# Moving half output maps of the S5 branch from GpSimd to VectorE, earlier, in a fused attention + SSM + FFN layer

## The chip, the cores and the metric

The kernel runs on one core of one Trainium2 chip. The metric is the device time of one execution in microseconds (us), as the median of several runs. The core has five engines that run side by side and meet only at semaphores: TensorE (PE, matmuls; its weight loads are listed as PEld), VectorE (DVE), ScalarE (ACT), GpSimd (POOL) and SyncE (SP, which here only issues DMAs).

## The reference

One layer of a hybrid encoder, 16 meta tokens ahead of 512 tokens, model width 1024, all in float32:

```python
xn = rmsnorm(h, norm1_g)
q, k, v, u, gates = split(xn @ w_in)          # 4 heads of 64; u is 512 wide; gates 2 x 1024
q, k = rmsnorm(q, q_norm_g), rmsnorm(k, k_norm_g)     # per head
attn = stick_breaking_attention(q, k, v)
y = s5_ssm(u, ...)                            # 32 groups of 16 channels, 64 complex states each
g = gelu(y); ssm = g * sigmoid(g @ w_glu + b_glu)
h = h + (sigmoid(gate_a) * (attn @ w_attn_proj) + sigmoid(gate_s) * (ssm @ w_ssm_proj)) @ w_o
up = causal_dwconv3(rmsnorm(h, norm2_g) @ w_up)
h = h + (silu(gate_f) * val_f) @ w_down       # FFN width 2816
```

The S5 recurrence is x[t] = A x[t-1] + B u[t], y[t] = Re(C x[t]) + D u[t], with A diagonal and complex.

## The kernel before

Tokens lie on the free axis, so an activation is stored as 8 tiles of 128 channels by 528 tokens. Every product with a weight matrix is done in three float32 products (high by high, high by low part, low by high) and cut into **units**: one unit is 128 output channels, 48 matmuls of 252 or 264 columns. Units 0 to 3 give u, 4 and 5 K, 6 and 7 Q, 8 and 9 V, 10 to 24 and 27 the gates, 25 and 26 the GLU, 28 to 35 the two projections, 36 to 43 W_o; the FFN follows. The weights go through two slots, even and odd units: SP loads `raw`, ACT rounds it to `hi` (L925), VectorE makes `lo` = `raw` - `hi` (L1309), and PE waits for `lo_ready` ahead of each unit. ACT may overwrite a slot of `hi` only when the unit two before is done, so `lo` of unit n+2 can be made only while unit n+1 runs on PE.

Each engine walks the same list of units. At unit n, VectorE first makes `lo` of unit n+2 (`split`) and then does the steps that `STEPS[n]` lists, in order; ACT first evacuates unit n, then rounds `hi` of unit n+2, then does its steps; PE runs unit n and then its steps; SP loads the weights of unit n+2 and then does `MOVES[n]`. No engine looks ahead: what stands behind a wait in its list waits as well. GpSimd has one list of its own, written out at the end of its block.

The S5 branch is worked in 4 rounds of 4 pairs of groups, in chunks of 8 tokens, beside units 8 to 16:

- the **input map** of a round (`g_in`, GpSimd, `input_map`) and its **output map** (`hout`, `map_part`), each with a real and an imaginary half. One half map is 3 multiplies or adds of 128x576 (L499, L500, L501) from the powers `pw` and from `ct`. There are three buffers `hout`, so the map of round 3 waits until round 0 has been read out
- `prep` r: PE turns the input map and multiplies the output map into the taps (waits `g_ready`, `h_pool`, `h_dve`); ACT copies `win` and `kern` (L1037, `kern_raw`); VectorE adds the skip term (L1507, `kern_set`); SP spreads the taps over `toep` in 8 DMAs (L540, `kern_out`)
- `state` r: PE (L1949), then VectorE's rotation and scan (L1528 to L1542), which sets `xst` (`st_set`)
- `readout` r: PE multiplies the taps (L1961) and the states (L1970); it waits for `kern_out`, for `st_set`, and for the last users of banks 6 and 7, which are the copy of `kern` and the two copies of V (`vl_set`, L1552) of `turn_v`. `y_ps` says that it is done

Before the change GpSimd makes the imaginary halves (`parts=(1,)`) of rounds 0, 1 and 2 and both of round 3; VectorE makes the real halves of rounds 0, 1 and 2 in units 6, 7 and 8 (the step `out_map`), with `mod` as scratch, for which it waits until all of u has been written (`u_out`). The step `norms` of unit 9 is, on VectorE, the Newton step of the q and k norms (L1315 to L1317, `rows_set`); SP's `norm_write` and `norm_read` of units 11 and 12 move its result, and `scale` uses it in unit 12. After its maps GpSimd makes masks and then restores the residual, `hT` times `rb` in 8 instructions (L892), for W_o.

Of the kernel before, what the change touches and what calls it, by code (L numbers as in the profile page):

```python
# [23 lines left out]
P = 128  # L24
# [7 lines left out]
KD = D // P  # L32
# [3 lines left out]
GROUPS, GH, ST = 32, 16, 64  # L36
# [8 lines left out]
T8 = 8  # L45
NC = L // T8
RP = PAIRS // 4
ROUNDS = 4
# [50 lines left out]


STEPS = {0: [("angle", 0)], 1: [("angle", 1)], 2: [("columns", 0), ("angle", 2)],
         3: [("turns", 0)], 4: [("columns", 1), ("turns", 1)],
         5: [("square", 0)], 6: [("square", 1), ("out_map", 0)],
         7: [("square", 2), ("out_map", 1)], 8: [("square", 3), ("out_map", 2), ("prep", 0)],
         9: [("state", 0), ("norms", 0)],
         10: [("prep", 1), ("turn_v", 0)], 11: [("readout", 0), ("state", 1)],
         12: [("prep", 2), ("turn_v", 1)] + [("scale", i) for i in range(4)], 13: [("readout", 1), ("state", 2)],
         14: [("prep", 3), ("turn_v", 2)], 15: [("readout", 2), ("state", 3), ("head", 0)],
         16: [("head", 1), ("readout", 3)],
# [18 lines left out]
NORM_TILE = 32  # L128
TURN_BANK = 7
HOUTS = 3  # L130


ROW_ARE, ROW_AIM, ROW_STEP, ROW_SKIP = 0, 32, 64, 96
# [33 lines left out]
def hybrid_trunk(nc, x, meta_tokens, norm1_g, w_in, q_norm_g, k_norm_g, ssm_a_re, ssm_a_im,  # L167
# [8 lines left out]
    with ctx:  # L176
        def alloc(stack, name, shape, dt=F32):
            return stack.enter_context(nc.sbuf_tensor(name, shape, dt))
# [4 lines left out]
        def sem(name):  # L183
            return ctx.enter_context(nc.semaphore(name))
# [31 lines left out]
        HOUT = 2 * RP * (T8 + 1) * GH  # L216
        v_at = hout_end - HOUTS * HOUT - 2 * L
        vT = [gates[:, v_at + i * L:v_at + (i + 1) * L] for i in range(2)]
# [5 lines left out]
        ma = [alloc(mix, f"ma{i}", [P, LL]) for i in range(2)]  # L224
        mb = [alloc(mix, f"mb{i}", [P, LL]) for i in range(2)]
        pad = alloc(mix, "pad", [P, 4 * (L - LL)])
        v2 = alloc(mix, "v2", [P, 5, HEADS, 2 * DH], F32R)
        skips = ExitStack()
        skip_i = alloc(skips, "skip_i", [GH, GROUPS, GH])
# [16 lines left out]
        mod = alloc(early, "mod", [P, 4, RP, NC])  # L246
# [9 lines left out]

        hout = [gates[:, hout_end - (HOUTS - i) * HOUT:hout_end - (HOUTS - 1 - i) * HOUT]
                .rearrange("p (c r n h) -> p c r n h", c=2, r=RP, h=GH) for i in range(HOUTS)]
        kern = alloc(early, "kern", [GH, 2 * RP, P])
# [100 lines left out]
        pw_set = sem("pw_set")  # L360
# [4 lines left out]
        h_pool = sem("h_pool")  # L365
        h_dve = sem("h_dve")
# [6 lines left out]
        u_out = [sem(f"u_out{i}") for i in range(ROUNDS)]  # L373
# [5 lines left out]
        st_set = sem("st_set")  # L379
        y_ps = sem("y_ps")  # L380
# [108 lines left out]
        def map_part(eng, link, r, c, t, n=RP):  # L489

            shape = [P, n, T8 + 1, GH]
            t = t[:, 0:n * (T8 + 1) * GH].rearrange("p (r n h) -> p r n h", r=n, h=GH)
            for r0 in range(0, RP, n):
                pr = slice(r * RP + r0, r * RP + r0 + n)
                a = [pw[:, i, :, pr].rearrange("p n r -> p r n").unsqueeze(3).broadcast_to(shape)
                     for i in range(2)]
                b = [ct[:, i, pr, :].unsqueeze(2).broadcast_to(shape) for i in range(2)]
                o = hout[r % HOUTS][:, c, r0:r0 + n]
                link(eng.tensor_tensor(o, a[0], b[c], ALU.mult))  # L499
                link(eng.tensor_tensor(t, a[1], b[1 - c], ALU.mult))  # L500
                link(eng.tensor_tensor(o, o, t, ALU.subtract if c else ALU.add))  # L501
# [8 lines left out]
        def linker(eng, link):  # L510

            count = [0]

            def wait_for(ins):
                count[0] += 1
                ins.then_inc(link, 1)
                eng.wait_ge(link, count[0])
            return wait_for
# [28 lines left out]
        def _(sp):  # L547
# [97 lines left out]
            def y_read(_):  # L645
                for r in range(ROUNDS):
                    sp.wait_ge(y_out[r], 16)
                sp.wait_ge(st_set, ROUNDS)
                sp.wait_ge(y_ps, ROUNDS)
                for g in range(2 * RP):  # L650
                    sp.dma_start(yT[GH * g:GH * (g + 1)].rearrange("p r j c -> p (r j) c"),
                                 y_dram[:, :, :, g].rearrange("r j h c -> h (r j) c"))\
                        .then_inc(y_in, 16)
# [9 lines left out]
            def rms_read(_):  # L663

                sp.wait_ge(rms_out, 32)
                sp.dma_start(rb[:], rms_dram.partition_broadcast(P)).then_inc(rb_in, 16)
# [66 lines left out]
        def _(pool):  # L733
            link = linker(pool, pool_link)
# [87 lines left out]
            def input_map(r):  # L822

                if r >= 2:
                    pool.wait_ge(g_t, r - 1)
                n = RP if r < 2 else RP // 2
                shape = [P, n, T8, GH]
                for r0 in range(0, RP, n):
                    pr = slice(r * RP + r0, r * RP + r0 + n)
                    cmul(pool, link, both(g_in[r % 2][:, :, r0:r0 + n]),  # L830
                         [pw[:, c, 0:T8, pr].rearrange("p n r -> p r n").unsqueeze(3)
                          .broadcast_to(shape) for c in range(2)],
                         [bb[:, c, pr, :].unsqueeze(2).broadcast_to(shape) for c in range(2)],
                         tmp(n, T8, GH))
                pool.nop().then_inc(g_ready, 1)

            def output_map(r, parts=(1,)):

                if r >= HOUTS:
                    pool.wait_ge(y_ps, r - HOUTS + 1)  # L840
                for c in parts:
                    map_part(pool, link, r, c, pt, RP if r < 2 else RP // 2)
                pool.nop().then_inc(h_pool, 1)

# [15 lines left out]
                             .broadcast_to([P, PAIRS, NC - 1])).then_inc(decay_set, 1)  # L860
            output_map(1)
            input_map(1)
            output_map(2)
            input_map(2)
            input_map(3)
            output_map(3, (0, 1))

            tri = pt[:, 0:P]
            link(pool.memset(tri, -1.0))
# [19 lines left out]

            pool.wait_ge(rb_in, 16)  # L890
            for k in range(KD):
                pool.tensor_tensor(hT[:, k, :], hT[:, k, :], rb[:], ALU.mult).then_inc(h_raw, 1)  # L892
            for m in range(KD):
                pool.wait_ge(m_gated, m + 1)
# [408 lines left out]
        def _(dve):  # L1303
            link = linker(dve, dve_link)
# [8 lines left out]
            def newton(r, v, t, factor=1.0):  # L1313

                link(dve.scalar_tensor_tensor(t, v, -0.5 * factor, r, ALU.mult, ALU.mult))  # L1315
                link(dve.tensor_tensor(t, t, r, ALU.mult))
                return dve.scalar_tensor_tensor(r, t, 1.5 * factor, r, ALU.add, ALU.mult)  # L1317
# [107 lines left out]
                dve.scalar_tensor_tensor(xl[:, k], hT[:, k], g1[:, k:k + 1], xh[:, k].bitcast(F32),  # L1425
                                         ALU.mult, ALU.subtract).then_inc(x_ready, 1)

            def out_map(r):

                if r >= HOUTS:  # L1430
                    dve.wait_ge(y_ps, r - HOUTS + 1)
                if r == 0:
                    dve.wait_ge(pw_set, 1)
                    for u in u_out:
                        dve.wait_ge(u, 16)
                map_part(dve, link, r, 0, mod_flat)
                dve.nop().then_inc(h_dve, 1)

            mod_flat = mod[:].rearrange("p i r c -> p (i r c)")

            def rounded(o, n):

# [43 lines left out]
                                                None, ALU.mult)  # L1486
                ins.then_inc(ct_set, 1)

            def norms(_):

                dve.wait_ge(rs_a, 1)
                newton(row_r, row_v, row_t).then_inc(rows_set, 1)
# [175 lines left out]
            def evacuate(unit):  # L1668
# [2 lines left out]
                dve.tensor_copy(*unit_tile(unit)).then_inc(gate_late, 1)  # L1671

            steps = {"columns": columns, "out_map": out_map, "angle": angle, "turns": turns,
                     "norms": norms, "scale": scale, "prep": prep, "state": state,
                     "head": head,
                     "scores": scores, "suffix": suffix, "values": values, "gelu": gelu,
                     "turn_v": turn_v}
# [131 lines left out]
        def _(pe):  # L1809
# [109 lines left out]
            def prep(r):  # L1919

                pe.wait_ge(g_ready, r + 1)
                for c in range(2):
                    for i in range(RP):
                        ins = pe.transpose(ps[:, 4 + c, i * P:(i + 1) * P],
                                           g_in[r % 2][:, c, i].rearrange("p j h -> p (j h)"), ident[:])
                ins.then_inc(g_t, 1)
                pe.wait_ge(h_pool, r + 1)
                pe.wait_ge(h_dve, min(r + 1, HOUTS))
                for k in range(RP // 2):
                    for c in range(2):  # L1930
                        for half in range(2):
                            i = 2 * k + half
                            p0 = ST * half
                            ins = pe.matmul(ps[p0:p0 + 3 * GH, 6, k * P:(k + 1) * P],
                                            bpair[:, c, r * RP + i, :],
                                            hout[r % HOUTS][:, c, i, 0:T8, :]
                                            .rearrange("p i h -> p (i h)"),
                                            start=c == 0, stop=c == 1)
                ins.then_inc(k_ps, 1)
# [333 lines left out]
            for half in range(2):  # L2273
                pe.wait_ge(lo_ready, U_END - 1 + half)
                for c in range(2):
                    t = slice(2 * P * c, 2 * P * (c + 1))
                    for i in range(UT):
                        k = half * UT + i
# [33 lines left out]
```

## Time and profile before

| | us |
|---|---|
| median of 3 runs (706.46, 706.69, 709.88) | 706.69 |
| the profiled execution | 707.04 |
| its span, first to last instruction | 705.3 |
| PE busy | 694.5 (98%) |
| VectorE busy | 422.4 (60%) |
| ScalarE busy | 322.0 (46%) |
| GpSimd busy | 184.3 (26%) |

The span is cut into 40 equal slices on the page; each digit is the busy share of a slice in tenths, and PEclk is the granted TensorE clock. The stretch of this case is slices 3 to 8, some 50 to 155 us.

```profile
PE   9999989989999999999999999999999999999998
DVE  5775989687777756445766666666666662322221
POOL 7899999920000023231101010101101010000000
```

Most of the chain that ended last is PE's products; the same page puts 90% of it on PE and 4% on VectorE.

### The profile page before, as it was taken

How to read it: one execution, taken by the hardware profiler on the slowest of the kernel's cores; microseconds unless marked ns; L12 is line 12 of the kernel's file. 1: busy time of each engine (PE TensorE's matmuls, PEld its weight loads, DVE VectorE, ACT ScalarE, POOL GpSimd, SP SyncE). 2: the span in 40 equal slices, each digit the busy share in tenths (PEclk: the TensorE clock that was granted, in tenths of full speed). 3: DMA queues.
4: the chain of work that ended last, by engine and by line, in shares of the span. 5: the costliest groups of instructions: out<-in, count | busy, mean ns of one | idle time of the engine just before them, and what ended most of it. 6: DMA issues, size and time to landing. Idle time of an engine off the chain costs nothing.

```text
span 705.3 us, 14227 instructions
## 1 busy us (share of the span) xinstructions
PE 694.5 (98%) x5680; PEld 662.4 (94%) x5680; DVE 422.4 (60%) x559; ACT 322.0 (46%) x483; POOL 184.3 (26%) x209
## 2 busy tenths in 40 slices
PE   9999989989999999999999999999999999999998
PEld 7899979989999999999999999999999998888887
DVE  5775989687777756445766666666666662322221
ACT  4754543668889653445444444444343432111220
POOL 7899999920000023231101010101101010000000
PEclk9999999999999999999999999999999999999999
DMA  8168344249211234333333333333333342333331
GB/s 232 47 186 135 78 124 135 64 139 114 70 60 53 68 91 121 90 91 90 90 91 90 89 89 89 91 91 99 98 96 90 100 124 82 98 97 97 97 98 46
DMA packets 139930, 69.26 MB, mean 98 GB/s; under 512 B 23476, under 2 KB 137880, under 8 KB 139888
## 3 DMA queue, kind: packets, MB, share of 16 engines
q1 hardware_dynamic: 139727, 68.65, 36.7%
q8 instruction: 30, 0.49, 0.3%
q14 instruction: 13, 0.10, 0.0%
q10 hardware_dynamic: 160, 0.02, 0.0%
HBM read 63.19 MB, written 4.28 MB: 96 GB/s over the span
## 4 chain that ended last, share of the span: by engine, by line
PE 90%; DVE 4%; ACT 2%; issue 2%; SPq 1%; DMA 1%; POOL 0%; DVEq 0%; ACTq 0%; POOLq 0%
PE ps L1814 80%; PE ps L1841 1%; PE ps L2017 1%; PE ps L2067 1%; PE ps L1865 1%; DVE lo L1309 1%; PE ps L1970 1%; PE ps L2034 1%; ACT xh L994 1%; PE ps L1961 1%; DVE mod L500 1%; SPq L540 1%; DVE gates L499 1%; DVE gates L501 1%; PE ps L1874 1%
## 5 line engine op out<-in xcount | busy, mean ns | idle before, releaser
L925 ACT ACTIVATE hi<-raw 128x1024 fp32r<-128x1024 f32 (+2 forms) x102 | 111.5, 1094 | 244.2 <-PE ps L1814 226.6
L1814 PE MATMUL ps<-xh,hi 128*128 128x264 f32 (+1 forms) x1088 | 219.5, 283 | 0.1
L1814 PE MATMUL ps<-xl,hi 128*128 128x264 f32 (+1 forms) x1088 | 218.7, 282 | 0.0
L1309 DVE TENSOR_TENSOR lo<-raw,hi 128x1024 fp32r<-128x1024 f32 (+2 forms) x102 | 135.5, 1328 | 138.9 <-ACT hi L925 138.3
L1814 PE MATMUL ps<-xh,lo 128*128 128x264 f32 (+1 forms) x1088 | 218.0, 282 | 0.0
L1814 PEld LDWEIGHTS ps<-xh,hi 128*128 128x128 f32 x1088 | 167.3, 189 | 1.5 <-issue 0.6
L1814 PEld LDWEIGHTS ps<-xl,hi 128*128 128x128 f32 x1088 | 166.8, 188 | 0.0
L1814 PEld LDWEIGHTS ps<-xh,lo 128*128 128x128 f32 x1088 | 166.6, 188 | 0.0
L908 POOL TENSOR_TENSOR cv<-cv 128x512 f32<-128x512 f32 x22 | 28.3, 1289 | 226.7 <-DVE cv L1766 226.7
L1814 PE MATMUL ps<-ah,hi 128*128 128x512 f32 (+1 forms) x198 | 74.3, 375 | 0.0
L1814 PE MATMUL ps<-al,hi 128*128 128x512 f32 (+1 forms) x198 | 73.1, 369 | 0.0
L1814 PE MATMUL ps<-ah,lo 128*128 128x512 f32 (+1 forms) x198 | 72.9, 368 | 0.0
L1766 DVE SCALAR_TENSOR_TENSOR cv<-ut,cols,cv 128x512 f32<-128x512 f32 x88 | 65.9, 749 | 7.6 <-DVE cv L1766 2.7
L1755 DVE TENSOR_TENSOR ut<-ps,rb 128x516 f32<-128x516 f32 x44 | 30.6, 695 | 61.4 <-PE ps L1814 61.3
L1814 PEld LDWEIGHTS ps<-ah,lo 128*128 128x128 f32 x198 | 37.2, 188 | 7.3
L895 POOL TENSOR_TENSOR ma<-ma,mb 128x516 f32<-128x516 f32 x8 | 10.9, 1359 | 125.2 <-DVE mb L1711 125.2
L1814 PEld LDWEIGHTS ps<-ah,hi 128*128 128x128 f32 x198 | 37.2, 188 | 6.6
L1814 PEld LDWEIGHTS ps<-al,hi 128*128 128x128 f32 x198 | 37.3, 188 | 6.5
L1254 ACT ACTIVATE cv<-ut,cols 128x512 f32<-128x512 f32 x44 | 35.6, 808 | 1.8 <-DVE ut L1755 1.6
L1261 ACT ACTIVATE cv<-cv 128x512 f32<-128x512 f32 x22 | 13.9, 633 | 34.5 <-DVE cv L1766 34.5
L1814 PE MATMUL ps<-mh,hi 128*128 128x264 f32 (+1 forms) x128 | 25.7, 282 | 0.5 <-DVE ml L1695 0.3
L1814 PE MATMUL ps<-ml,hi 128*128 128x264 f32 (+1 forms) x128 | 25.8, 283 | 0.0
(298 smaller groups left out, 956.0 us busy)
## 6 DMA issues: line engine op xcount, KB each, us to landing
raw<-in_w_up_dram SPq DMA_DIRECT2D x88, 256.0 KB, 3.1
raw<-in_w_in_dram SPq DMA_DIRECT2D x52, 256.0 KB, 3.4
raw<-in_w_down_dram SPq DMA_DIRECT2D x16, 384.0 KB, 3.5
raw<-in_w_down_dram SPq DMA_DIRECT2D x16, 320.0 KB, 4.0
raw<-in_w_o_dram SPq DMA_DIRECT2D x16, 256.0 KB, 3.0
xtok<-in_x_dram SPq DMA_DIRECT2D x4, 512.0 KB, 5.5
raw<-in_w_ssm_proj_dram SPq DMA_DIRECT2D x8, 256.0 KB, 2.8
out_dram<-yt SPq DMA_DIRECT2D x7, 256.0 KB, 2.4
```

Source lines behind the costliest of these rows:

```text
L499: link(eng.tensor_tensor(o, a[0], b[c], ALU.mult))
L500: link(eng.tensor_tensor(t, a[1], b[1 - c], ALU.mult))
L501: link(eng.tensor_tensor(o, o, t, ALU.subtract if c else ALU.add))
L895: pool.tensor_tensor(ma[m % 2][:], ma[m % 2][:], mb[m % 2][:], ALU.add)\
L908: pool.tensor_tensor(cv[s][:, 1], cv[s][:, 0], cv[s][:, 1], ALU.mult)\
L925: act.activation(hi[slot][:, 0:n * P], raw[slot][:, 0:n * P], ACT.Copy)\
L1254: act.activation(cv[s][:, part], ut[s][:, part, 2:2 + SEQ], ACT.Identity, bias=cols[:, bass.ds(m + COL_CB, 1)], scale=cols[:, bass.ds(m + ...
L1261: act.activation(cv[s][:, 0], cv[s][:, 0], ACT.Silu).then_inc(silu_a, 1)
L1309: dve.tensor_tensor(lo[slot][:, 0:n * P], raw[slot][:, 0:n * P], hi[slot][:, 0:n * P].bitcast(F32), ALU.subtract)\
L1755: dve.tensor_tensor(ut[s_][:, part], joined(4 * s_ + 2 * part, CUT_LATE), rb[:, 0:LL], ALU.mult).then_inc(up_v, 1)
L1766: dve.scalar_tensor_tensor(cv[s_][:, part], ut[s_][:, part, 2 + tap:2 + tap + SEQ], w, cv[s_][:, part], ALU.mult, ALU.add)\
L1814: ins = pe.matmul(o, weights[w], acts(a, c), start=start and i == 0, stop=stop and i == 2)
```

## The change

It moves work between engines and within VectorE's list; what is computed stays the same.

- VectorE makes four half maps instead of three: the real halves of rounds 0, 1 and 2 and the imaginary half of round 2. They stand in units 4, 5, 6 and 7 instead of 6, 7 and 8. The scratch is a new tile `map_tmp` in the place where `v2` (the turned V) lies later, so the wait for `u_out` is gone.
- GpSimd makes the imaginary halves of rounds 0 and 1 and both of round 3. `output_map(2)` is gone from its list.
- PE's waits in `prep` follow that split (`POOL_MAPS`, `DVE_MAPS`).
- VectorE's Newton step of the norms, now called `rates`, moves from unit 9 (behind `state` 0) to unit 10, behind `prep` 1 (the taps' skip term) and `turn_v` 0.
- GpSimd's residual restore waits for `st_set` of all four rounds ahead of its fifth instruction.

```diff
-         3: [("turns", 0)], 4: [("columns", 1), ("turns", 1)],
-         5: [("square", 0)], 6: [("square", 1), ("out_map", 0)],
-         7: [("square", 2), ("out_map", 1)], 8: [("square", 3), ("out_map", 2), ("prep", 0)],
+         3: [("turns", 0)], 4: [("columns", 1), ("turns", 1), ("out_map", 0)],
+         5: [("square", 0), ("out_map", 1)], 6: [("square", 1), ("out_map", 2)],
+         7: [("square", 2), ("out_map", 3)], 8: [("square", 3), ("prep", 0)],
          9: [("state", 0), ("norms", 0)],
-         10: [("prep", 1), ("turn_v", 0)], 11: [("readout", 0), ("state", 1)],
+         10: [("prep", 1), ("turn_v", 0), ("rates", 0)], 11: [("readout", 0), ("state", 1)],
+MAPS_HERE = ((0, 0), (1, 0), (2, 0), (2, 1))
+MAPS_THERE = {0: (1,), 1: (1,), 3: (0, 1)}
+DVE_MAPS, POOL_MAPS = (1, 2, 4, 4), (1, 2, 2, 3)
+        maps = ExitStack()
+        map_tmp = alloc(maps, "map_tmp", [P, RP * (T8 + 1) * GH])
+        maps.close()
         v2 = alloc(mix, "v2", [P, 5, HEADS, 2 * DH], F32R)
...
-            def output_map(r, parts=(1,)):
+            def output_map(r):
...
-                for c in parts:
+                for c in MAPS_THERE[r]:
                     map_part(pool, link, r, c, pt, RP if r < 2 else RP // 2)
...
             output_map(1)
             input_map(1)
-            output_map(2)
             input_map(2)
             input_map(3)
-            output_map(3, (0, 1))
+            output_map(3)
...
             for k in range(KD):
+                if k == KD // 2:
+                    pool.wait_ge(st_set, ROUNDS)
                 pool.tensor_tensor(hT[:, k, :], hT[:, k, :], rb[:], ALU.mult).then_inc(h_raw, 1)
...
-            def out_map(r):
-                if r >= HOUTS:
-                    dve.wait_ge(y_ps, r - HOUTS + 1)
-                if r == 0:
-                    dve.wait_ge(pw_set, 1)
-                    for u in u_out:
-                        dve.wait_ge(u, 16)
-                map_part(dve, link, r, 0, mod_flat)
+            def out_map(i):
+                r, c = MAPS_HERE[i]
+                dve.wait_ge(pw_set, 1)
+                map_part(dve, link, r, c, map_tmp)
                 dve.nop().then_inc(h_dve, 1)
...
-            def norms(_):
+            def rates(_):
                 dve.wait_ge(rs_a, 1)
                 newton(row_r, row_v, row_t).then_inc(rows_set, 1)
...
-                pe.wait_ge(h_pool, r + 1)
-                pe.wait_ge(h_dve, min(r + 1, HOUTS))
+                pe.wait_ge(h_pool, POOL_MAPS[r])
+                pe.wait_ge(h_dve, DVE_MAPS[r])
```

## Rows read from the trace of the kernel before

**Rows 1.** Waits of PE, whole span: us in total, times, longest.

```profile
PE ps L1961 <- issue: 2.9, 1, 2.9
```

**Rows 2.** Windows: start:end, length, busy us of each engine, PEclk, DMA.

```profile
102.40:107.30 4.90, 4.90 (x129) 4.58 (x129) 1.01 (x1) 1.88 (x3) 4.41 (x6) 0.65 0.81 241
121.30:124.70 3.40, 3.40 (x130) 3.16 (x129) 2.68 (x3) 0.63 (x2) 3.16 (x4) 1.00 0.02 5
```

**Rows 3.** Timeline, end of unit 11: start, duration, instruction, [idle before <- releaser].

```profile
98.40 1.52 ACT L1037 ACTIVATE kern<-ps 16x256 f32<-16x256 f32 x4
99.56 1.74 DVE L1309 TENSOR_TENSOR lo<-raw,hi 128x1024 fp32r<-128x1024 f32 x1
101.22 0.72 DVE L1507 TENSOR_TENSOR kern<-kern,skip_i 16x128 f32<-16x128 f32 x1
101.87 0.41 DVE L1552 TENSOR_TENSOR v<-ps,v 128x256 fp32r<-128x256 f32 x1
102.38 1.66 PE L1961 MATMUL ps<-uc,toep 128*64 128x66 f32 x32 [2.90 <-issue]
```

**Rows 4.** Timeline, SP's queue, ACT and VectorE ahead of that.

```profile
86.60 5.61 SPq L540 DMA_DIRECT2D toep<-kern  x8
92.25 2.24 SPq L556 DMA_DIRECT2D raw<-in_w_in_dram  x4
96.25 1.25 DVE L1315 SCALAR_TENSOR_TENSOR gates<-gates 128x528 f32<-128x528 f32 x1
96.48 1.06 ACT L925 ACTIVATE hi<-raw 128x1024 fp32r<-128x1024 f32 x1 [4.35 <-DMA raw<-in_w_in_dram]
```

**Rows 5.** Timeline, VectorE, units 4 to 7.

```profile
57.49 1.12 DVE L1471 TENSOR_SCALAR rot<-rot 128x1056 f32<-128x1056 f32 x1
59.85 2.19 DVE L1309 TENSOR_TENSOR lo<-raw,hi 128x1024 fp32r<-128x1024 f32 x1 [1.25 <-ACT hi L925]
65.50 1.53 DVE L1309 TENSOR_TENSOR lo<-raw,hi 128x1024 fp32r<-128x1024 f32 x1 [3.46 <-ACT hi L925]
72.13 2.21 DVE L1309 TENSOR_TENSOR lo<-raw,hi 128x1024 fp32r<-128x1024 f32 x1 [0.15 <-DVE gates L501]
```

**Rows 6.** Windows from first to last instruction of two of VectorE's half maps.

```profile
66.95:71.98 5.03, 5.03 (x44) 5.03 (x43) 4.96 (x4) 2.17 (x4) 4.87 (x4) 1.00 0.20 23
81.26:85.90 4.64, 4.64 (x69) 3.81 (x68) 4.54 (x4) 1.87 (x4) 4.30 (x4) 1.00 0.01 4
```

**Rows 7.** Timeline, PE: first matmul of units 7, 8 and 9.

```profile
63.71 0.28 PE L1814 MATMUL ps<-xh,hi 128*128 128x252 f32 x1
69.42 0.29 PE L1814 MATMUL ps<-xh,hi 128*128 128x264 f32 x1
77.25 0.39 PE L1814 MATMUL ps<-xh,hi 128*128 128x264 f32 x1
```

**Rows 8.** Timeline: `state` 2 and 3 on VectorE, GpSimd's restore, `readout` 3.

```profile
127.22 0.70 DVE L1528 TENSOR_TENSOR mod<-ps,rot 128x528 f32<-128x528 f32 x1
132.29 0.77 DVE L1542 TENSOR_TENSOR xst<-mod 128x260 f32<-128x260 f32 x2
134.33 11.54 POOL L892 TENSOR_TENSOR hT<-hT,rb 128x528 f32<-128x528 f32 x8
142.20 0.71 DVE L1528 TENSOR_TENSOR mod<-ps,rot 128x528 f32<-128x528 f32 x1 [0.28 <-PE ps L1949]
149.02 0.77 DVE L1542 TENSOR_TENSOR xst<-mod 128x260 f32<-128x260 f32 x2
149.94 1.16 PE L1961 MATMUL ps<-uc,toep 128*64 128x66 f32 x32 [1.86 <-DVE xst L1542]
```

**Rows 9.** SP's taps of round 3 (timeline); DMA view, last of them: KB, landing.

```profile
141.12 6.18 SPq L540 DMA_DIRECT2D toep<-kern  x8
toep<-kern SPq DMA_DIRECT2D x1, 8.0 KB, 1.8
```

**Rows 10.** Timeline, SP's queue: the taps of round 1.

```profile
107.51 5.22 SPq L540 DMA_DIRECT2D toep<-kern  x8
```

More of the change, by code:

```diff
@@ L1426, in _ @@
                                          ALU.mult, ALU.subtract).then_inc(x_ready, 1)
-            def out_map(r):
-                if r >= HOUTS:
-                    dve.wait_ge(y_ps, r - HOUTS + 1)
-                if r == 0:
-                    dve.wait_ge(pw_set, 1)
-                    for u in u_out:
-                        dve.wait_ge(u, 16)
-                map_part(dve, link, r, 0, mod_flat)
+            def out_map(i):
+                r, c = MAPS_HERE[i]
+                dve.wait_ge(pw_set, 1)
+                map_part(dve, link, r, c, map_tmp)
                 dve.nop().then_inc(h_dve, 1)
-            mod_flat = mod[:].rearrange("p i r c -> p (i r c)")
             def rounded(o, n):
@@ L1673, in _ @@
             steps = {"columns": columns, "out_map": out_map, "angle": angle, "turns": turns,
-                     "norms": norms, "scale": scale, "prep": prep, "state": state,
+                     "rates": rates, "scale": scale, "prep": prep, "state": state,
                      "head": head,
```

## The prediction

> **What bounds the kernel now.** The page first: PE is busy 98% of the span and carries 90% of the chain that ended last, so an edit on VectorE or GpSimd can only win back stalls of PE, or add some. Then the waits of PE, for where it stood still, then the timeline on both sides of each stall. From 33 us on there are two stalls of weight. The first is 2.90 us ahead of `readout` 0, end of unit 11 at 102.38 - 2.90 = 99.48 [rows 1, 3]. The profile names no releaser ("issue"); the reader finds it by the last of the awaited events: VectorE's copy of V ends at 101.87 + 0.41 = 102.28, and PE starts at 102.38 [rows 3]. The idle has a tail: behind it the granted clock averages 0.65, so part of the time was at the lower level of 1.2 GHz, and the same 130 matmuls take 4.9 us from 102.4 against 3.4 us from 121.3 at full clock [rows 2]. That is 1.5 us more. The second stall is 1.86 us ahead of `readout` 3, on `xst` [rows 8]. No clock loss is seen there. The two are worth 2.9 + 1.5 + 1.9 = 6.3 us, 0.9% of the time: all that this change can win.
>
> **Why the first stall is there.** Read backwards [rows 3, 4]: the copy of V stands behind `lo` of unit 12 (99.56) and the skip term (101.22) on VectorE. VectorE was in the Newton step from 96.25 to 99.56, 3.3 us. ACT's `hi` of unit 12 came at 96.48, since its weights are loaded behind the eight taps' DMAs of round 0 in SP's queue (86.60 to 92.2), and these waited for VectorE's skip term of round 0, which stood behind the third half map. So two edits aim at this stall: maps ahead of unit 8, Newton step behind the copy.
>
> **The change, part by part.** I count from T8, the start of unit 8 on PE, 69.42 before [rows 7].
>
> *Half maps in units 4 to 7: new stalls.* A half map of VectorE takes 5.03 us, the fastest 4.64 [rows 6], with GpSimd busy all the time (4.87 and 4.30 in those windows); GpSimd's list up to `output_map(2)` is unchanged, so it is busy in units 4 to 7 too, and I take 5.03. The map of unit 4 starts when `turns` ends, 57.49 + 1.12 = 58.61, and ends at 63.68. Behind it in VectorE's list is `lo` of unit 7, which before ran from 59.85 to 62.04. Now it starts at 63.8 (0.15 behind a map [rows 5]) and lasts 1.53 to 2.21, I take 1.9: end 65.7. PE wants it at 63.71 [rows 7]. **PE stalls 2.0 us.** Next: the map of unit 5 (5.03), 0.15, `lo` of unit 8 (1.9) make 7.1 less the 0.05 by which neighbours overlap; unit 7 takes 69.42 - 63.71 = 5.71. **PE stalls 1.3 us more**, and T8 becomes 72.8, 3.4 later. Unit 8 with `prep` 0 behind it takes 77.25 - 69.42 = 7.83 [rows 7], longer than 7.1, so unit 9 does not wait, nor does unit 10, with the norms' and the state's products behind unit 9. With the shortest durations the two stalls are 1.3 + 0.5 = 1.8, with the longest 2.4 + 1.6 = 4.0. A gain is excluded: `lo` of unit 7 cannot be earlier than before.
>
> The GPSIMD Engine Reference of the Trainium skill (Key points) says that GpSimd shares its SBUF interfaces with VectorE, where VectorE's instruction has two SBUF inputs; the maps are of that kind, and the rows agree: an instruction of a map, 128x576, takes a third of 5.03 us, with GpSimd busy, while L1528, which reads PSUM, takes 0.70 on 528. By VectorE: DVE Perf Modes of the Trainium skill (Specifications), 0.96 GHz at an element per cycle, a map alone would be 3 x 0.6 = 1.8 us and neither stall would come; no run here shows a map alone.
>
> *First stall.* VectorE's list behind T8: map of unit 6, `lo` 9, map of unit 7, `lo` 10, skip term: 5.0 + 2.0 + 5.2 + 1.8 + 0.6 = 14.6, so the taps' DMAs start at T8 + 14.6 (before: 86.60 - 69.42 = 17.2). The rest of the chain keeps its price from there: `hi` of unit 12 at +9.9 (96.48 - 86.60), `kern` copied at +13.3 (98.40 + 1.52 - 86.60), then the V copies, 0.9: T8 + 28.8. `state` 0 ends by T8 + 25.6, with `lo` 12 (1.7) and the skip term (0.7) that is T8 + 28.0, the Newton step no longer among them. PE ends unit 11 at T8 + 99.48 - 69.42 = T8 + 30.1. So the stall of 2.90 and the 1.5 of clock go, with 1.2 us in hand. Gain 4.4.
>
> *Newton step moved.* It still issues three instructions, 3.3 us. It now ends at T8 + 32.2, 104.9 against 99.6 before. Behind it: on VectorE `lo` 13, which PE wants at the end of unit 12 (+39.6), and `state` 1, which starts when PE has its product (+33.6), so nothing. On SP, `norm_write`, the load of unit 14, `norm_read` and the taps of round 1 all slide by 5.3: these start at 107.51 + 5.3 = 112.8 [rows 10], take 5.2, land 1.8 after the last issue, 119.3. `readout` 1 is due at T8 + 33.6 + (121.3 - 107.3) = 120.4. Covered by 1.1 us; if not, it is at most a few tenths to 1.
>
> *GpSimd.* It loses one half map (six instructions), and all after it comes some 5 us earlier, less what VectorE's longer work slows it. No stall of PE names GpSimd, so this is worth nothing there.
>
> *Restore in two parts.* `state` 3 takes 142.20 to 149.79, 7.59 us, with GpSimd's restore (134.33 to 145.87) over its first half; `state` 2, without it, takes 127.22 to 133.06, 5.84 [rows 8]. Now the first four multiplies end well before `state` 3 and the others wait for it, so it ends 1.75 earlier, 148.04 in the old times, where PE is free at 149.94 - 1.86 = 148.08. But the taps of round 3 are late next: their DMAs start at 141.12 with the end of `readout` 2 and move with PE; the last is issued at about 141.12 + 6.18 - 0.57 = 146.7 and lands 1.8 later, 148.5 [rows 9]. About 0.5 us of the stall stays. Gain 1.35, between 0.9 and 1.86. The other four multiplies then run beside `head` and `lo` of unit 18, needed a unit later; GpSimd's own users of them are in W_o: nothing.
>
> **Sum.** +3.4 - 4.4 - 1.35 = -2.35, bounds -4.4 and -1.3. Against the profiled execution: 707.04 - 2.35 = 704.7, span 703.0. That one ran 0.35 above the median of the runs shown, so 706.69 - 2.35 = **704.3**.
>
> **Rivals.**
> *No new stalls* (12%): the maps run at VectorE's lone speed or overlap less. Then -4.4 - 1.35 = -5.75: 700.9. Against it: GpSimd has no pause in that stretch.
> *The clock falls after the stall of unit 7* (10%). An idle of 2.90 was followed by a half clock, one of 1.86 was not [rows 2, 8]; mine is 2.0. TensorE: Matmul & The Clock Gate of the Trainium skill (What's actually happening) makes the throttled state the default that activity lifts, which the fall after the first stall agrees with. A fall costs some 1.9 us of dense matmuls (a clock of 0.65 over 4.9 us loses 1.7), but it lengthens unit 7 and so hides the 1.3 of the next stall: about +0.6, 704.9; with a fall after unit 8's instead, 706.2.
> *The taps of round 1 come late* (10%): +0.5 to +1, 705.1.
> *Slower than before: the first stall stays* (7%). If the weights of unit 12 land over 1.2 us later than counted, PE waits again at `readout` 0. At 3.6 us late the kernel equals the old one; with the whole 2.9 and its clock back it is +3.4 - 1.35 = +2.05: 708.7. For it: one chain of SP, DMA, ACT and VectorE in a row; against: each of its links is priced by this very chain.
>
> **How the numbers follow.** Forecast 61%, 702.4 to 705.4. The range for 8 in 10 reaches down towards the first rival and up over the clock and tap cases: 701.4 to 706.6. What this kernel's measurement can tell from no change is 0.5%, 3.5 us: faster than 703.15 holds the first rival and the short end of the forecast, 29%; slower than 710.2 would need two of the bad cases together, 4%; 67% lies within.
>
> **What would show it.** In the trace of the changed kernel: a stall of PE ahead of L1814 in unit 7 of some 2 us and one in unit 8 of some 1.3, both released by `lo` L1309, which directly follows L501. No idle ahead of `readout` 0, its 130 matmuls in 3.4 us at clock 1.0, and the copy L1552 ahead of L1315. `state` 3 in about 5.9 us, and an idle of about 0.5 ahead of `readout` 3 with no VectorE releaser. Wrong if L499 to L501 take under 1.2 us each in units 4 and 5, if `hi` of unit 12 comes over 11 us behind the first taps' DMA, or if PE's clock drops near 66 us.

## The result: slower by 0.3%

| | before | after |
|---|---|---|
| median, us | 706.91 (706.22 to 712.23) | 709.87 (707.15 to 712.44) |
| profiled execution, us | 707.04 | 708.54 |
| its span, us | 705.3 | 706.8 |
| its mean granted clock | 0.998 | 0.998 |

The ratio is 1.0031, with a 95% interval of 1.0018 to 1.0044: slower, by 3.0 us in the medians. The forecast was 2.35 us faster, with a range that ended at 706.6. The account below is of the two profiled executions, +1.5 us. The other 1.5 us of the medians is not in it: the changed kernel's median lies 1.3 above its profiled execution, and where the clock fell in the executions without a trace is not shown.

Waits of PE in the changed kernel (engine, tile, line, releaser: us in total, times, longest), those that lie between unit 7 and `suffix` 0:

```profile
PE ps L1962 <- issue: 2.3, 1, 2.3
PE ps L1815 <- DVE lo L1316: 2.0, 1, 2.0
...
PE ps L1962 <- DMA toep<-kern: 0.3, 1, 0.3
PE ps L2035 <- DVE awl L1576: 0.3, 1, 0.3
...
PE ps L2018 <- issue: 0.2, 1, 0.2
```

The stall of 2.9 us ahead of `readout` 0 [rows 1] is gone. There is a stall of 2.0 us in unit 7, as forecast, none in unit 8, and one of 2.3 us ahead of `readout` 1 that the forecast did not have. Its timeline (start, duration, instruction, idle before and releaser), PE's first matmul of units 7 and 8 and of `readout` 0, 1 and 3:

```profile
66.05 0.39 PE L1815 MATMUL ps<-xh,hi 128*128 128x252 f32 x1 [2.04 <-DVE lo L1316]
73.42 0.32 PE L1815 MATMUL ps<-xh,hi 128*128 128x264 f32 x1
...
103.42 1.16 PE L1962 MATMUL ps<-uc,toep 128*64 128x66 f32 x32
...
123.20 1.16 PE L1962 MATMUL ps<-uc,toep 128*64 128x66 f32 x32 [2.28 <-issue]
...
150.21 1.16 PE L1962 MATMUL ps<-uc,toep 128*64 128x66 f32 x32 [0.26 <-DMA toep<-kern]
```

Set beside the same matmuls of before, the two kernels stand to each other like this (PE's start after, less its start before; of the events without a row the numbers are from the same timelines; `scores` 0 and `suffix` 0, L2018 and L2035, are PE's first two steps of the attention, q times k and the running sums):

| event | before | after | difference |
|---|---|---|---|
| unit 7 | 63.71 | 66.05 | +2.3 |
| unit 8 | 69.42 | 73.42 | +4.0 |
| `readout` 0 | 102.38 | 103.42 | +1.0 |
| unit 12, behind it | 107.21 | 106.74 | -0.5 |
| `readout` 1 | 121.34 | 123.20 | +1.9 |
| `readout` 3 | 149.94 | 150.21 | +0.3 |
| `scores` 0 | 157.96 | 158.62 | +0.7 |
| `suffix` 0 | 165.68 | 166.83 | +1.2 |
| end | 705.3 | 706.8 | +1.5 |

Up to unit 12 the forecast holds: +4.0 where it said +3.4, then -4.5 where it said -4.4. Of the 2.3 of unit 7, 2.0 is the stall and 0.3 comes from the first 35 us, where the traces of all kernels differ by some tenths. Two things come behind it. At `readout` 1 the kernel loses 2.3 us. At `readout` 3 it wins 1.6, as it should, and gives 0.9 of that back at `scores` 0 and `suffix` 0.

**Unit 7 and 8.** Windows (start:end, length, busy us of PE, PEld, DVE, ACT, POOL, then PEclk, DMA share, GB/s): behind the stall of unit 7, and over `readout` 0.

```profile
66.00:70.00 4.00, 3.95 (x20) 3.95 (x21) 3.93 (x3) 0.22 (x1) 3.83 (x3) 0.59 0.52 132
102.00:107.00 5.00, 5.00 (x143) 4.66 (x142) 3.88 (x5) 3.44 (x4) 4.69 (x5) 1.00 0.03 9
```

PE is busy for 3.95 of the 4 us of the first window, yet gets only 20 matmuls done, at a mean clock of 0.59: most of it at the lower level of 1.2 GHz. Unit 7 so ends late enough that `lo` of unit 8 is there. The loss is 1.7 us in place of a stall of 1.3: that is the clock rival. In the second window the clock is 1.00, where before had 0.65 [rows 2].

VectorE's side of the first stall: the map starts behind `turns`, and `lo` of unit 7 behind the map.

```profile
57.63 1.13 DVE L1472 TENSOR_SCALAR rot<-rot 128x1056 f32<-128x1056 f32 x1
58.80 1.56 DVE L505 TENSOR_TENSOR gates<-pw,ct 128x576 f32<-128x576 f32 x1
...
62.16 1.67 DVE L507 TENSOR_TENSOR gates<-gates,map_tmp 128x576 f32<-128x576 f32 x1
63.99 2.01 DVE L1316 TENSOR_TENSOR lo<-raw,hi 128x1024 fp32r<-128x1024 f32 x1 [0.15 <-DVE gates L507]
```

The map takes 63.83 - 58.80 = 5.03 us, exactly the value taken from [rows 6], and `lo` 2.01 for the 1.9 assumed.

**`readout` 1: the wait that was not in the forecast.** From the end of the Newton step to PE's start:

```profile
101.64 0.70 DVE L1322 SCALAR_TENSOR_TENSOR gates<-gates 128x528 f32<-128x528 f32 x1
...
104.60 1.16 SPq L679 DMA_DIRECT2D norm_dram<-gates  x4
107.72 5.06 SPq L689 DMA_DIRECT2D gates<-norm_dram  x8
112.91 5.99 SPq L546 DMA_DIRECT2D toep<-kern  x8
120.22 1.54 ACT L1044 ACTIVATE kern<-ps 16x256 f32<-16x256 f32 x4 [4.94 <-DMA toep<-kern]
121.79 0.49 DVE L1508 TENSOR_TENSOR kern<-kern,skip_i 16x128 f32<-16x128 f32 x1 [4.33 <-ACT kern L1044]
122.41 0.69 DVE L1553 TENSOR_TENSOR v<-ps,v 128x512 fp32r<-128x512 f32 x1
```

The taps' DMAs start at 112.91 (forecast 112.8). They land at 120.2 at the latest, 0.9 later than counted, but about when PE is due (120.9 = 123.20 - 2.28): that was not the loss. The loss is behind them. There is one buffer `kern` for all rounds, and `prep` of the next round, which stands ahead of `turn_v` 1 on both engines, may not write it before round 1's taps have left it. In ACT's `prep`:

```
if r:
    act.wait_ge(kern_out[r - 1], 16 * T8)
```

So ACT stands for 4.94 us, released by the DMA `toep<-kern`. Then come its four copies (1.54), VectorE's skip term and only then the copy of V, for which PE waits: 3.0 us behind the landing, from 120.2 to 123.2. PE's own record says "issue" here, as it did for the old first stall. The releaser is found one engine further up.

**`readout` 3 and behind it.** `state` 3 has its 5.8 us (144.06 to 149.83), and 0.26 us of the stall is left, released by the taps' DMA. But the weights of unit 18 are loaded behind these taps in SP's queue:

```profile
142.99 5.89 SPq L546 DMA_DIRECT2D toep<-kern  x8
149.91 7.55 POOL L899 TENSOR_TENSOR hT<-hT,rb 128x528 f32<-128x528 f32 x4 [17.18 <-DVE xst L1543]
150.59 3.41 DVE L1567 TENSOR_TENSOR ql<-qT,qh 64x516 fp32r<-64x516 f32 x2
153.69 1.06 ACT L932 ACTIVATE hi<-raw 128x1024 fp32r<-128x1024 f32 x1 [3.11 <-DMA raw<-in_w_in_dram]
157.90 0.61 ACT L1061 ACTIVATE yg<-ps 128x528 f32<-128x528 f32 x1
```

ACT waits 3.11 us for the weights. Its `hi` of unit 18 comes 2.4 us later than before (151.32), its gelu copy 2.4 later (155.53) and ends at 158.51, and PE starts `scores` 0 at 158.62. VectorE's split of the head is also slow, 3.41 us beside GpSimd's last four multiplies. Before, no multiply ran beside it:

```profile
150.56 1.39 DVE L1566 TENSOR_TENSOR ql<-qT,qh 64x516 fp32r<-64x516 f32 x2
```

So two causes stood open for what is given back.

### The profile page after: what moved, and what is told of

It is laid out like the page before. It is cut to its first block, busy times and chain, and to the rows that moved or that the text cites. A ratio compares the mean times of both kernels' runs of the same rounds, so it can differ in the third digit from the quotient of the medians.

```text
span 706.8 us, 14222 instructions
## 1 busy us (share of the span) xinstructions
PE 694.9 (98%) x5680; PEld 661.9 (94%) x5680; DVE 426.7 (60%) x562; ACT 321.9 (46%) x483; POOL 179.0 (25%) x203
## 4 chain that ended last, share of the span: by engine, by line
PE 81%; DVE 6%; ACT 5%; SPq 4%; issue 2%; DMA 2%; POOL 0%; DVEq 0%; ACTq 0%
PE ps L1815 74%; SPq L546 2%; DVE lo L1316 1%; DMA raw<-in_w_in_dram 1%; DVE gates L505 1%; DVE gates L507 1%; DVE map_tmp L506 1%; PE ps L2068 1%; PE ps L1866 1%; ACT hi L932 1%; PE ps L2035 1%; PE ps L2018 1%; ACT xh L1001 1%; DMA xtok<-in_x_dram 1%; SPq L689 1%
```

## The experiments

The theories. **Taps**: the Newton step, moved behind the copy of V, delays the taps of round 1, which costs 2 us through the buffer `kern`. **Splits**: what is given back after `readout` 3 comes from GpSimd's multiplies beside VectorE's splits; its rival is **loads**: it comes from SP's order. **Map**: the stall of unit 7 (and 8, or its clock) comes from the map in unit 4 alone. Ratios are against the kernel before, run on the same chip, whose median there is given behind the slash.

### One part undone or alone

**The Newton step back in unit 9**, all else as changed:

```
-         9: [("state", 0), ("norms", 0)],
-         10: [("prep", 1), ("turn_v", 0), ("rates", 0)], ...
+         9: [("state", 0), ("norms", 0), ("rates", 0)],
+         10: [("prep", 1), ("turn_v", 0)], ...
```

> The changed kernel with VectorE's Newton step of the norms back in unit 9, behind state 0, as before the change; all else as changed. Taps theory: the new 2.3 us stall of PE ahead of readout 1 comes from the Newton step's late end (rows_set at 104.6), which holds SP's norm moves and behind them the taps of round 1, whose landing ACT's copy of kern for round 2 waits for. Here rows_set comes at about 101.9 or earlier, the taps of round 1 start no later than 110 instead of 112.9, and the stall ahead of readout 1 is under 0.5 us. In exchange the copy of V stands 3.3 us later again (101.7 + 3 = 104.7 against PE's 103.4): a stall of about 1.4 us ahead of readout 0. Span about 706. Rival theory (state 1 or GpSimd's contention makes readout 1 late): the stall of 2.3 us stays, readout 0 waits 1.4 as well, span about 708.2.

Measured 707.7 / 707.1, ratio 1.0005 [0.9992, 1.0017]; span 706.2 at clock 1.0. Waits of PE, and the start of round 1's taps:

```profile
PE ps L1815 <- DVE lo L1316: 3.2, 2, 1.9
PE ps L1962 <- issue: 1.3, 1, 1.3
...
109.99 5.13 SPq L546 DMA_DIRECT2D toep<-kern  x8
```

No stall is left ahead of `readout` 1; one of 1.3 us is back ahead of `readout` 0. The taps start 2.9 us earlier. The clock did not fall here, and the two stalls of units 7 and 8 show themselves: 1.90 and 1.28 us, where the forecast had 2.0 and 1.3.

**The Newton step moved alone**, in the kernel before (`norms` split in two, `rates` put behind `turn_v` 0 in unit 10):

> The kernel before with only the Newton step moved to unit 10 behind turn_v 0; maps and restore as before. Taps theory: readout 0 still waits, as the maps are not moved, but 1.3 us instead of 2.9, with no or little lost clock behind it; readout 1 then waits some 2.5 to 3 us, since rows_set comes at about 104 instead of 99.6; span 704.5 to 706.5, so no clear gain. Rival theory (the stall at readout 1 needs the moved maps): no stall at readout 1, span about 702.5.

Measured 712.31 / 707.1, ratio 1.0065 [1.0029, 1.0101]; its six executions spread from 709.10 to 716.15, and the profiled one took 714.27, span 712.6. A miss, by 6 us: the worst kernel of the study.

```profile
PE ps L1961 <- DVE v L1552: 4.8, 1, 4.8
PE ps L1961 <- ACT kern L1037: 2.8, 1, 2.8
PE ps L1961 <- issue: 1.9, 1, 1.9
...
130.58 12.54 POOL L892 TENSOR_TENSOR hT<-hT,rb 128x528 f32<-128x528 f32 x8
140.54 2.86 DVE L1542 TENSOR_TENSOR xst<-mod 128x260 f32<-128x260 f32 x2
```

Three stalls, ahead of `readout` 0, 1 and 2. The first stays, since `hi` of unit 12 is late without the earlier maps; the 1.9 ahead of `readout` 1 is the taps' again. The large one is new. `state` 2, shifted by the delay, now falls in with GpSimd's eight multiplies: it takes 13.4 us (130.02 to 143.4) in place of 5.84. Its last two instructions, which write `xst` (L1542), take 2.86 together in place of 0.77 [rows 8], its two scans (L1534, L1535) 1.70 and 1.76 in place of 0.71 and 0.73. PE waits 4.8 us for the copy of V behind it, and the clock is 0.50 in the 4 us that follow. The restore in two parts does not only help `state` 3, then. It guards `state` 2 from an earlier restore as well, which the forecast gave no value.

**The restore in two parts alone**, in the kernel before:

```
  for k in range(KD):
+     if k == KD // 2:
+         pool.wait_ge(st_set, ROUNDS)
```

> The kernel before with only the residual restore in two parts. State 3 takes 5.9 us instead of 7.6, the stall ahead of readout 3 shrinks from 1.9 to about 0.5 (the taps' DMAs of round 3 last), and the question is what is left of it. Give-back theory: the four late multiplies stretch VectorE's head splits, and the weights of unit 18 keep ACT's last gelu copy and the first softmax where they were, so PE waits again at scores 0 and suffix 0 and the span falls by 0.5 us or less. Rival theory: the gain of 1.4 us stays, span 703.9.

Measured 707.17 / 707.1, ratio 0.9999 [0.9983, 1.0015]. Its profiled execution (span 707.4) stands 2.9 us behind at the end of unit 11, with a mean clock of 0.84 in its first 22 us where the trace of before has 1.00; the edit touches nothing there. Set against that, it wins 1.8 us at `readout` 3, loses 0.8 again by `suffix` 0 and 0.4 in small differences up to the end: 0.5 net. So the gain comes, and is largely given back, without any of the other edits.

**Round 1's taps ahead of the norms' DMAs**, all else as changed. In SP's list:

```
-         11: [("norm_write", 0)],
-         12: [("norm_read", 0), ("toep", 1), ("y_write", 0)],
+         12: [("toep", 1), ("norm_write", 0), ("norm_read", 0), ("y_write", 0)],
```

> The changed kernel with SP's moves reordered: the taps of round 1 stand ahead of norm_write and norm_read, all in unit 12. Taps theory: the taps of round 1 start at about 105.7 with the end of readout 0 instead of 112.9, ACT's copy of kern is not held, and the stall of 2.3 us ahead of readout 1 is gone; the norms land about 4 us later, which VectorE's scale in unit 12 waits for without a stall of PE. Span about 704.5 with the stall and clock fall of unit 7 as in the changed kernel. Rival theory: readout 1 waits for VectorE's state 1 or V copy anyway, stall over 1.5 us, span 706.8.

Measured 706.62 / 707.1, ratio 0.9993 [0.998, 1.0005]; span 704.9, against 706.8 for the changed kernel, and 704.5 expected.

```profile
105.74 5.58 SPq L545 DMA_DIRECT2D toep<-kern  x8
...
PE ps L1814 <- DVE lo L1315: 2.0, 1, 2.0
PE ps L1961 <- DMA toep<-kern: 0.5, 1, 0.5
```

The taps start 7.2 us earlier, nothing is idle ahead of `readout` 0 or 1, and the Newton step stands where the change put it. With the first kernel of this section this shows the taps' theory from both sides: the step costs nothing where it stands on VectorE, what it delays in SP's queue does. That the delay passes through the buffer `kern` is read from ACT's wait; a second such buffer was not tried.

### The maps, and both together

**The first map in unit 3**, all else as changed. There VectorE is ahead of its splits:

```
-         3: [("turns", 0)], 4: [("columns", 1), ("turns", 1), ("out_map", 0)],
+         3: [("turns", 0), ("out_map", 0)], 4: [("columns", 1), ("turns", 1)],
```

> The changed kernel with VectorE's first half map in unit 3 instead of unit 4, where VectorE waits 5.8 us for ACT anyway; the other maps stay in units 5, 6 and 7. Stall theory: lo of unit 7 is made at about 60 again, the map of unit 5 ends before lo of unit 8 is wanted, so PE waits neither in unit 7 nor in unit 8 and its clock has no reason to fall there: unit 8 starts at 69.5 instead of 73.4 and all after it 3.9 us earlier, with the 2.3 us stall ahead of readout 1 still there. Span 702.9. Rival theory (GpSimd's contention, not the order in VectorE's list, makes lo late): a stall of 1 us or more stays in unit 7 or 8, span 705.

> The kernel with the first map in unit 3 and with the taps of round 1 ahead of the norm moves in SP's queue. Both theories add up: no stall in units 7 and 8, none ahead of readouts 0 and 1; what is left is 0.5 us ahead of readout 3 and the small waits at scores 0 and suffix 0. Span 700.9, time about 702.6, 0.6% under the kernel before. Rival: a new wait ahead of readout 1 or 2, since the norms land late and VectorE's scale waits for them: span 702.5.

The first measured 706.43 / 707.07, ratio 0.9991 [0.9979, 1.0003], span 704.0 where 702.9 was expected. Units 7 and 8 have no idle, and the clock stays at 1.00: what the map cost is gone. With all of it earlier, the delay at `readout` 1 meets GpSimd's first four multiplies in `state` 2:

```profile
PE ps L1962 <- issue: 3.2, 2, 1.9
...
128.38 6.90 POOL L899 TENSOR_TENSOR hT<-hT,rb 128x528 f32<-128x528 f32 x4
134.12 1.78 DVE L1543 TENSOR_TENSOR xst<-mod 128x260 f32<-128x260 f32 x2
```

The two waits are 1.9 us ahead of `readout` 1 (2.3 expected) and 1.4 ahead of `readout` 2 (none expected), which makes most of the 1.1 by which it missed. The second kernel has the taps' order as well: 703.19 / 707.07, ratio 0.9946 [0.9927, 0.9965], span 701.7 where 700.9 was expected. 5.1 us of span are won over the changed kernel by two edits of order alone. A wait of 1.0 ahead of `readout` 2 (the same overlap: the last pair of `state` 2 takes 1.90) and one of 0.7 ahead of `readout` 3 are left.

### Splits or loads

Two kernels go on from this one. The first moves the restore out of the scan, between GpSimd's sums in the projections. The second also puts the weights ahead of the taps on SP (`toep` 0 one unit later, `toep` 3 from unit 15 to 16).

```
+RESTORE = {0: (0, 1), 1: (2, 3), 2: (4,), 3: (5,), 4: (6,), 5: (7,)}
...
+                for k in RESTORE.get(m, ()):
+                    pool.tensor_tensor(hT[:, k, :], hT[:, k, :], rb[:], ALU.mult).then_inc(h_raw, 1)
```

> The kernel with both of these and GpSimd's residual restore taken out of the S5 stretch altogether: its eight multiplies stand between the gated sums of the projections. If GpSimd's late multiplies beside VectorE's head splits cause the waits at scores 0 and suffix 0, these go: heads' splits take 0.7 us each instead of 1.7, and the span falls by 1.2 us to 699.7. If the late weights of unit 18 and ACT's gelu copy cause them, the waits stay and the span is 700.7 or so.

> The kernel with the late restore and, in SP's queue, the taps of rounds 0 and 3 behind the weight loads of units 12 and 18 instead of ahead of them. hi of unit 18 comes some 6 us earlier, ACT's gelu copy of round 3 and its first softmax pass are not held, so the waits at scores 0 and suffix 0 (together 1.2 us in the changed kernel) are gone; the 0.5 us ahead of readout 3 stay. Span 699.5 against 700.7 without this edit, if ACT's chain was the cause; the same as without it, if VectorE's was.

Measured 708.11 / 707.07, ratio 1.0016 [1.0005, 1.0026], and 706.06 / 707.07, ratio 0.9983 [0.9972, 0.9995]; spans 707.6 and 704.4. Both missed their totals, as the multiplies in the projections hold up GpSimd's other work there, and VectorE's sums behind it:

```profile
PE ps L1813 <- DVE mb L1710: 3.8, 3, 1.9
...
243.37 3.33 POOL L901 TENSOR_TENSOR hT<-hT,rb 128x528 f32<-128x528 f32 x2
```

That is 3.8 us of stalls, in the second kernel 1.92, 0.88 and 1.04, and in both the clock falls behind the first of them (0.62 and 0.58 over 4 us). The question they were made for they do answer. At `readout` 3 the first stands 4.9 us ahead of the kernel before, and waits of 0.7 at `scores` 0 and 0.3 at `suffix` 0 remain, although no multiply runs near the splits: it gives 1.3 us back. The second stands 6.6 us ahead there and keeps all of it; both waits are gone. Loads, not splits. Only those 1.3 us are the loads': the 1.7 between the two kernels at `readout` 3 is there by unit 9 already, and comes from a mean clock of 0.92 in the first 22 us of the first kernel's trace, 1.00 in the second's.

**All orders, the restore in two parts left in the scan**:

```
-         7: [("rms_write", 0)], 8: [("rms_read", 0)], 9: [("toep", 0)],
+         7: [("rms_write", 0)], 8: [("rms_read", 0)], 10: [("toep", 0)],
...
-         15: [("toep", 3)], 16: [("y_write", 2)], ...
+         16: [("toep", 3), ("y_write", 2)], ...
```

> The changed kernel with the first map in unit 3 and SP's queue in the new order (taps of rounds 0 and 3 behind the loads of units 12 and 18, taps of round 1 ahead of the norm moves), the restore in two parts as in the change. The late restore between the gated sums cost some 5.6 us, all of it in the projections; up to readout 3 the kernel was 6.6 us ahead. So this one keeps that lead, less what GpSimd's four late multiplies beside the head splits cost: nothing, if it was the late weights of unit 18 that had made the waits at scores 0 and suffix 0 (span 699.0, 0.9% faster than before); up to 1.2 us, if it was the stretched splits (span 700.2).

Measured **701.88** / 706.84, ratio 0.9937 [0.9914, 0.9961], span 699.3 at clock 1.0 where 699.0 was expected: the best kernel of the study, faster than the kernel before and so than the changed one (1.0031). One of its six executions took 706.30, at a mean clock of 0.995; why is not shown.

```profile
PE ps L1961 <- DMA toep<-kern: 0.3, 1, 0.3
...
144.11 1.05 ACT L931 ACTIVATE hi<-raw 128x1024 fp32r<-128x1024 f32 x1
144.22 3.43 DVE L1566 TENSOR_TENSOR ql<-qT,qh 64x516 fp32r<-64x516 f32 x2
148.30 0.62 ACT L1060 ACTIVATE yg<-ps 128x528 f32<-128x528 f32 x1
```

0.3 us of waiting is left in the whole scan, and the 6.0 us by which PE is ahead at `readout` 3 last to the end. The wait ahead of `readout` 2 is gone too, which the expectation did not name, so that part is luck: GpSimd's first multiply starts at 130.77, and `state` 2 has ended at 129.50. The splits of the head are as slow as in the changed kernel, 3.43 us, and nobody waits for them; `hi` of unit 18 no longer waits for a DMA.

**The whole restore behind attention**:

> As c1, but all eight multiplies of the restore wait until the attention is done (about 225 us) and run beside the GLU. Nothing of GpSimd's stretches state 2, state 3 or the head splits; the first gated sum comes at about 241, when the eight (9 to 11 us) are done. Span 698.9 if the GLU has room for it, one or two us more if VectorE's products of the GLU are on PE's path.

Measured 708.08 / 706.84, ratio 1.0009 [0.9998, 1.002]: a miss by 7.6 us of span (706.5 for 698.9).

```profile
PE ps L1814 <- DVE sl L1665: 2.9, 1, 2.9
PE ps L1814 <- DVE lo L1315: 2.2, 1, 2.2
...
223.50 14.83 POOL L898 TENSOR_TENSOR hT<-hT,rb 128x528 f32<-128x528 f32 x8 [95.16 <-PE ps L2067]
```

14.8 us of multiplies beside VectorE's products and splits there delay them in turn, and the clock falls behind the second stall (0.57 over 4 us; 1.00 behind the first). Of the three placements tried with the new order (one run here, spread over the projections, two parts in the scan) only the two parts cost nothing.

**The maps as before, all else as in the best kernel**:

> The kernel before with its own half maps (three on VectorE in units 6, 7 and 8, five on GpSimd), but with the Newton step moved, the restore in two parts and SP's queue in the new order. If the move of the maps has a worth of its own, it shows here: readout 0 no longer waits, so PE is 4.5 us earlier, and then GpSimd's last map, which ended at 128.8 before, is late for the taps of round 3, which PE wants at about 126: a stall of 2 to 2.8 us there, released by GpSimd, and a span near 701.5. Rival (only SP's order and the Newton step matter, where the maps are made does not): no stall there, span 699 as c1.

Measured 703.24 / 706.84, ratio 0.9953 [0.9935, 0.997], span 701.5, as expected to the tenth. One wait is new:

```profile
PE ps L1935 <- POOLq L842: 2.4, 1, 2.4
```

It is released by GpSimd, whose `output_map` ends late. So the four half maps on VectorE in units 3 to 7 are worth 2.2 us of span (701.5 to 699.3) once the rest is in order, 1.4 in the medians (703.24 to 701.88).

**The changed kernel once more**:

> The changed kernel once more, unaltered, to see which of its waits repeat and what the clock does behind them. The waits come from the order of the lists, so they repeat: about 2.0 us ahead of unit 7 and, with the clock up in unit 7, 1.3 us ahead of unit 8 (with the clock down, none there), nothing ahead of readout 0, about 2.3 us ahead of readout 1. The clock is the part that varies: after each of the two waits it falls in some executions and not in others, and each fall costs 1.5 to 2 us, which is how the median can lie 1.3 us above the profiled execution (708.54) and its runs spread over 5 us. If the clock's fall behind unit 7 were a fixed property of that wait, this profile would show it again and a median equal to the profiled time.

Measured 709.82 / 708.24, ratio 1.0023 [1.0007, 1.004], profiled 708.75. The windows view of the same stretch behind the stall of unit 7:

```profile
66.00:70.00 4.00, 3.48 (x29) 3.48 (x30) 3.93 (x4) 0.81 (x3) 3.83 (x3) 1.00 0.54 132
```

Here the clock is 1.00. The stalls are 1.93 in unit 7, 1.29 in unit 8 and 2.10 ahead of `readout` 1. So the stalls repeat and the clock does not: it fell behind 2.04 us and held behind 1.93. The fall and the second stall cost nearly the same, 1.7 and 1.3 us, so the profiled times are 708.54 and 708.75. Against the kernel before on the same chip the median is 1.6 us longer here, 3.0 in the first measurement.

## Why the prediction was wrong, step by step

**Right.** *Half maps in units 4 to 7: new stalls*: 1.93 and 1.29, or 1.90 and 1.28 us where the clock held, for 2.0 and 1.3; with a clock that fell, 2.04 and 1.7 us of clock. The rival *the clock falls after the stall of unit 7*, given 10%, came true in the profiled execution, with its mechanism (it hides the second stall) and nearly its price (+0.6 forecast; unit 8 starts at 73.42 where 72.8 was forecast). (In the forecast's bounds the longest first stall comes to 2.3 from its own rows and the shortest to 1.2, where it has 2.4 and 1.3; the sums hold.) *First stall*: gone, 4.5 for 4.4, at full clock. *GpSimd*: no stall names it. *Restore in two parts*, as far as `readout` 3: `state` 3 takes 5.8 us for 5.84, and the taps' DMA leaves 0.3 for 0.5.

**Wrong: *Newton step moved*, "Covered by 1.1 us; if not, it is at most a few tenths to 1".** The shift of SP's queue was right to 0.1 us (112.91 for 112.8), and the step failed at the question who waits for the landing. It named PE alone. The landing also frees `kern` for ACT, and behind ACT's copies stand VectorE's skip term and the copy of V: PE starts 3.0 us behind the landing. The price of the first stall was worked out over this same chain; the step for round 1 was not. Cost: 2.3 us in place of 0. The rival *the taps of round 1 come late* had the place right and the size wrong, 0.5 to 1. The runs show it by taking it away in two ways (Newton step back: no stall ahead of `readout` 1; taps first: none either, span 1.9 us shorter).

**Wrong: *Restore in two parts*, "the other four multiplies ... nothing. Gain 1.35".** The gain at `readout` 3 was 1.6, but the step stopped there. PE came earlier to `scores` 0, and what was late next had not been asked for: `hi` of unit 18, behind the taps of round 3 in SP's queue. 0.9 us were given back by `suffix` 0, and the small later differences belong here as well, as far as the runs tell: the best kernel has neither. Alone, the edit nets 0.5 us. That the multiplies would stretch a split of VectorE to 3.4 us was overlooked too, but it costs nothing (best kernel). Not seen either was what the two parts are worth besides: with the Newton step moved and no second wait, the eight multiplies fall over `state` 2 and PE waits 4.8 us.

**The sum, as it came out** in the profiled execution: +4.0 (for +3.4; 2.0 of stall, 1.7 of clock, 0.3 from the first 35 us), -4.5 (for -4.4), +2.3 (for 0), -1.6 (for -1.35), +0.9 (for 0), and some 0.4 in small differences later on: +1.5. That is 3.8 us above the 704.7 forecast for that execution, and the two wrong steps make 3.2 of it. The median, 709.87 for 704.3, is another 1.7 further off, and for that no cause is shown. The clock rival was given 10% and a single fall; one of the two traces of the changed kernel has it, and 14 of its 30 executions have a mean clock under 0.997, against 32 of the 82 executions of the kernel before that stand beside the experiments, which had a stall to fall behind too. The rival that ended slower, *the first stall stays*, did not occur: the forecast of the sign failed on terms that it had put at nothing. 701.4 to 706.6 was too narrow, since each of the two chains that were moved was followed to its first user alone, and the range had no term for a second.

The GPSIMD Engine Reference of the Trainium skill (Key points) names GpSimd's SBUF interfaces as shared with VectorE, for instructions of VectorE with two SBUF inputs. The trace of the Newton step moved alone agrees: beside GpSimd's multiplies VectorE's last pair of `state` 2 (L1542), which reads SBUF twice, went from 0.77 us [rows 8] to 2.86, the product L1529, which reads PSUM and SBUF, kept its 0.69, and the multiplies themselves took 12.54 / 8 = 1.57 us each.

## What to carry to other kernels

When a step slides in a queue, list every semaphore that its last instruction raises, and who waits for each: a buffer that is used again in the next round makes a waiter that stands on another engine, with its own chain behind it. A stall removed is a gain only as far as the next late event; follow the earlier start until nothing waits. And an edit on a compute engine can be right while the queue of DMAs that follows it is not: here two reordered lists turned +0.3% into -0.6%.

## What the runs showed of the hardware

**A clock that the length of the idle does not tell.** Behind an idle of 2.04 us (changed kernel) and 2.01 us (taps first) TensorE's clock fell to a mean of 0.59 and 0.69 in the next 4 us. Behind 1.93 and 1.90 us at the same place, and 2.10 and 2.28 ahead of `readout` 1, it stayed at 1.00. Nor does the length decide elsewhere: behind 1.92 us in the projections it fell in both kernels that had it (0.62 and 0.58), behind 2.43 us (maps as before) it stayed at 1.00. What decides is not shown. TensorE: Matmul & The Clock Gate of the Trainium skill (Part 1) calls the start-up behaviour variable from run to run. The traces agree, with a mean clock in the first 22 us of 1.00 in most and of 0.84 and 0.92 in two. A profiled execution thus shows one of several histories, and the difference between them is as large as the effect that was measured: in the 20 executions of the changed kernel the median span is 706.4 us where the mean clock was 0.999 or more (3 of them) and 708.7 where it was below 0.997 (9).

**Two busy neighbours.** Where GpSimd's multiplies met VectorE's work on SBUF, both stretched: the four late multiplies of the changed kernel took 7.55 us, 1.9 each, against 1.3 (5.16 / 4) for the first four of the best kernel, beside which VectorE is idle for most of the time; and a split of two instructions took 3.41 in place of 1.39. The same eight multiplies stood in every kernel; where they were put moved the time from 701.88 us (two parts in the scan, best kernel) to 708.08 (behind attention, all else the same).
